# A two-way recurrent scan on TensorE: same-half products in halves of 32 stationary columns, keys and values turned by quadrants

## The chip, the cores and the metric

The kernel runs on one core of a Trainium2 chip. The metric is the device time in microseconds, the median of several runs of the whole program. Inputs and outputs are fp32.

## What is computed

The reference is a chain of four layers on 256 tokens of width 1024: attention and a feed-forward layer, an RWKV-7 time mix and a mixture of experts, latent attention with retention, a gated linear attention, with feed-forward layers between. Only the time mix is touched, and of it the scan: 16 heads of 64 x 64 state, run over 272 tokens forwards and backwards.

```python
def _wkv7_step(S, inp):
    r, w, k, v, kk, a = inp
    sa = jnp.einsum('bhvk,bhk->bhv', S, kk)
    S = S * w[:, :, None, :] - sa[..., None] * (kk * a)[:, :, None, :] + v[..., None] * k[:, :, None, :]
    y = jnp.einsum('bhvk,bhk->bhv', S, r)
    return S, y
...
    _, y_fwd = lax.scan(_wkv7_step, S0, (r_t, tm(decay[0]), tm(kd[0]), v_t, kk_t, tm(a[0])))
    _, y_bwd = lax.scan(_wkv7_step, S0, (r_t, tm(decay[1]), tm(kd[1]), v_t, kk_t, tm(a[1])), reverse=True)
```

## The kernel before

Each engine has a program of its own, written out in full by a Python function (scan_pe, scan_act, scan_dve) with waits on semaphores by hand. The order on an engine is the order in which these functions issue. In the scan, `streams` interleaves three generators on every engine: direction 0, direction 1 and the bonus term, one step of each in turn. The names in the views are tiles: `scan_t` holds the prepared keys and decays and the states, `ring` the work tiles of direction 0, `arena` those of direction 1, `ps` is PSUM, `con` the constants.

The scan is done in chunks of 64 tokens: direction 0 has a first chunk of 16 and four of 64, direction 1 four of 64. Inside a chunk the recurrence is a triangular system. It is solved by doubling: levels 1 to 5 (1 to 3 in the chunk of 16), each with products T (L1454), Y (L1463, not in the last level) and X (L1469). What else TensorE does for a chunk:

- G (L1425): products of keys with keys and queries, in two groups; after the first group Vt (L1434), the values turned from features x tokens to tokens x features by a product with the identity.
- Ut (L1440), then BKt (L1447), the keys of both kinds turned in the same way.
- Z: L1475 within the chunk, and in chunks after the first L1483, which adds the state's part to the same PSUM regions.
- N (L1489), the new values; L1500, the state's part of the output; L1507, the new state; L1515, the output within the chunk.

Sixteen heads are eight tiles i of 128 partitions with two heads p each, head p in partitions 64p to 64p+63. A product of one head uses 64 rows of the array (the half its input is in) and 64 columns (the half its output goes to). `HEADS` is the order i, i+4 with both p; `part(j, i)` sends tiles 4 to 7 to the other half, so that four consecutive products of T, Y, Z's L1475 and N use the four pairs of row half and column half. In X (L1469), L1483 and L1500 input and output are in the same half, so two pairs alternate. Vt and BKt use all 128 rows: one product turns the two heads of a tile, with 64 stationary columns (tokens) and the 128 columns of the identity moving.

`psum.take` deals PSUM banks in turn, aligned to the number asked for. ScalarE copies T, Z, N, Vt and BKt out of PSUM (L1601, L1606, L1612, L1588, L1595), VectorE masks and merges G, Y and X (L1706, L1728, L1732). Every fp32 product is two pairs of a weight load and a matmul record in the trace. The weights of the next stage come through the SP queue, and none of these DMAs stands in the scan.

Of the kernel before, what the change touches and what calls it, by code (L numbers as in the profile page):

```python
# [416 lines left out]
def build(nc, x_d, ws_d, par_d, con_d, dis_d, scn_d, rel_d, ow_d, moe_d, pos_d, out_d):  # L417
# [4 lines left out]
    with ctx:  # L422
# [38 lines left out]
        PS = ps_t[:, :, :]  # L461
# [4 lines left out]
        def con(n):  # L466
            return con_t[:, cc[n][0]:cc[n][0] + cc[n][1]]
# [30 lines left out]
        psum = Banks()  # L498
# [810 lines left out]
        SAME = [(i, p) for i, p in HEADS if i // 4 != p]  # L1309
        OTHER = [(i, p) for i, p in HEADS if i // 4 == p]  # L1310
        TILES = [i + 4 * x for i in range(4) for x in range(2)]

        def own(p, n=64):
            return slice(64 * p, 64 * p + n)

        def part(j, i, n=64):
            return own(j ^ (i // 4), n)
# [7 lines left out]
        def bank(b, i):  # L1325
            return b + i // 4
# [61 lines left out]
        def window(d, j, i, c0):  # L1388
            a = j * AB + i * T0 + c0
            return d.flat[:, a:a + 64]  # L1390

        def scan_pe(w, e):
            w.wait_ge(ac["project"], IN_SCN)

            def steps(n):
                d = dirs[n]
# [15 lines left out]
                for ci, (c0, cn) in enumerate(d.chunks):  # L1412
# [3 lines left out]
                    for q in range(2):  # L1416
# [12 lines left out]
                        if q == 0:  # L1429
                            b, free = psum.take(("Vt", *u))  # L1430
                            w.wait_ge(*free)
                            for i in TILES:
                                x = 128 * (i % 4)
                                last = e.matmul(PS[part(1, i), b, x:x + 128], Vr[:, i, c0:c0 + 64], con("ident"), start=True, stop=True)  # L1434
                            last.then_inc(*pe.on("Vt", *u))
# [8 lines left out]
                    for j in range(2):  # L1444
                        for i in TILES:
                            x = 128 * (i % 4)
                            last = e.matmul(PS[part(j, i), bank(b, i), x:x + 128], window(d, j, i, c0), con("ident"), start=True, stop=True)  # L1447
                    last.then_inc(*pe.on("BKt", *u))
                    yield
                    for lv in range(1, levels(cn)):  # L1450
# [17 lines left out]
                        for i, p in HEADS:  # L1468
                            last = e.matmul(spread(PS[own(p), b:b + 2, :], lv)[:, i], d.T[own(p, cn), i, :], side(d.X[own(p, cn), i, :], lv, d.x_side), start=True, stop=True)  # L1469
# [6 lines left out]
                    if ci:  # L1476
                        last.then_inc(*pe.on())
                        across = pe.now()
                        w.wait_ge(dv["S", n, ci - 1])
                        for i, p in SAME + OTHER:  # L1480
                            if (i, p) == OTHER[0]:
                                w.wait_ge(across)
                            last = e.matmul(PS[own(p, cn), bank(b, i), col(i)], d.AR[own(p), 0, i, cs], d.S[own(p), i, :], start=False, stop=i % 4 == 3)  # L1483
# [14 lines left out]
                    if ci:  # L1498
                        for i, p in STRAIGHT:
                            last = e.matmul(PS[own(p), bank(by, i), col(i, cn)], d.S[own(p), i, :], d.AR[own(p), 1, i, cs], start=i % 4 == 0, stop=False)  # L1500
                        last.then_inc(*pe.on())
                        straight = pe.now()
# [44 lines left out]
        def scan_act(w, e):  # L1547
            w.wait_ge(IN_SCN, IN_PAR)

            def steps(n):  # L1550
# [32 lines left out]
                for ci, (c0, cn) in enumerate(d.chunks):  # L1583
                    u = (n, ci)
                    w.wait_ge(pe["Vt", *u])
                    real = sn("rows")[:, int(cn < C):int(cn < C) + 1]
                    for x in range(2):
                        e.activation(d.NV[own(1 - x), 8 * x:8 * x + 8, :].rearrange("q i t -> q (i t)"), PS[own(1 - x), psum["Vt", *u], :], ACT.Identity, scale=real[own(1 - x)]).then_inc(*ac.on())  # L1588
# [6 lines left out]
                    e.activation(d.BKt.rearrange("q (x i) p t -> q x (i p t)", x=2), PS[:, b:b + 2, :], ACT.Copy).then_inc(*ac.on("BKt", *u))  # L1595
# [2073 lines left out]
```

## Time and profile before

| | us |
|---|---|
| median of 3 runs (lowest, highest) | 2608.56 (2607.54, 2610.41) |
| span of the profiled execution, first to last instruction | 2600.0 |
| TensorE busy, whole span | 2505.0 |
| the scan on TensorE, first product of a chunk to the last | 560 to 795 |
| TensorE, VectorE, ScalarE busy in 616.7 to 782.2 us | 157.95, 85.72, 63.71 |

The profile is of one execution, whose span is 2600.0 us; the runs' times are those of the whole launch and 8.6 us longer in the median. TensorE's busy time is the union of its matmul records, which overlap, so a busy engine may still take short bursts faster or slower. Idle time of an engine is given with what ended it; "issue" means that the profile shows nothing that it waited for. [...]

### The profile page before, as it was taken

The page shows a single profiled execution, that of the slowest core. Times are in us where ns is not written, and L with a number is a line of the kernel's source. Part 1 is how long each engine was busy: PE and PEld are TensorE (multiplying, and loading weights), DVE is VectorE, ACT ScalarE, POOL GpSimd, SP SyncE. Part 2 cuts the span into 40 slices and gives each one's busy share as a digit, 9 for nine tenths or more (in the row PEclk, how much of TensorE's full clock was granted, in tenths as well). Part 3 has the DMA queues.
Part 4 walks back from the last instruction along what each step waited for, and adds up shares of the span by engine and source line. Part 5 has one row for each costly group of instructions (what it writes and reads, how often), then busy time and mean ns, then how long its engine had stood idle before and what let it go on. Part 6 is the DMA issues. An engine that isn't in the chain of part 4 may idle for free.

```text
span 2600.0 us, 54588 instructions
## 1 busy us (share of the span) xinstructions
PE 2505.0 (96%) x23472; PEld 2331.7 (90%) x23472; DVE 1998.4 (77%) x3066; ACT 1537.2 (59%) x2510; POOL 51.9 (2%) x57
## 2 busy tenths in 40 slices
PE   8999999989999999999999999999898899999999
PEld 8779998868887899999999999999897799998999
DVE  5555547775544799999999999999877788675884
ACT  4435434464432677777777777777666566564663
POOL 0001100000000000000000000000003000000000
PEclk9999999978999999999999999999999999998999
DMA  6223452300003599999999999999732255541453
GB/s 246 73 74 122 178 190 100 107 1 4 20 4 115 206 376 337 367 340 368 341 366 335 372 337 370 335 373 345 287 139 105 78 192 191 188 173 50 171 181 128
DMA packets 83257, 538.46 MB, mean 207 GB/s; under 512 B 9488, under 2 KB 9616, under 8 KB 38976
## 3 DMA queue, kind: packets, MB, share of 16 engines
q1 hardware_dynamic: 82368, 530.68, 55.2%
q8 instruction: 186, 3.05, 0.5%
q0 software_dynamic: 640, 4.22, 0.4%
q14 instruction: 63, 0.52, 0.1%
HBM read 533.81 MB, written 1.05 MB: 206 GB/s over the span
## 4 chain that ended last, share of the span: by engine, by line
PE 87%; DVE 7%; ACT 4%; issue 1%; DMA 1%; DVEq 0%; SPq 0%; PEldq 0%; ACTq 0%
PE ps L576 23%; PE ps L577 23%; PE ps L578 23%; PE ps L1469 2%; DVE sl L534 2%; PE ps L591 1%; PE ps L582 1%; PE ps L2000 1%; PE ps L1463 1%; PE ps L1447 1%; PE ps L1454 1%; DMA ring<-ws_d 1%; PE ps L2145 1%; PE ps L1425 1%; PE ps L819 1%
## 5 line engine op out<-in xcount | busy, mean ns | idle before, releaser
L2227 DVE TENSOR_TENSOR sl<-ring,sh 128x1024 fp32r<-128x1024 f32 x613 | 718.1, 1219 | 13.5 <-ACT sh L2185 10.6
L2185 ACT ACTIVATE sh<-ring 128x1024 fp32r<-128x1024 f32 x613 | 609.0, 1061 | 1.3 <-DVE xl L2070 1.3
L576 PE MATMUL ps<-sh,xh 128*128 128x256 f32 (+2 forms) x2012 | 568.0, 282 | 2.1 <-DVE sl L534 1.2
L578 PE MATMUL ps<-sh,xl 128*128 128x256 f32 (+2 forms) x2012 | 567.5, 282 | 0.0
L577 PE MATMUL ps<-sl,xh 128*128 128x256 f32 (+2 forms) x2012 | 567.0, 282 | 0.0
L576 PE MATMUL ps<-xh,sh 128*128 128x256 f32 (+2 forms) x1856 | 538.5, 290 | 22.8 <-DVE sl L534 12.7
L577 PE MATMUL ps<-xl,sh 128*128 128x256 f32 (+2 forms) x1856 | 531.2, 286 | 0.0
L578 PE MATMUL ps<-xh,sl 128*128 128x256 f32 (+2 forms) x1856 | 529.0, 285 | 0.0
L534 DVE TENSOR_TENSOR sl<-ring,sh 128x1024 fp32r<-128x1024 f32 (+1 forms) x341 | 401.0, 1201 | 74.6 <-ACT sh L527 74.3
L527 ACT ACTIVATE sh<-ring 128x1024 fp32r<-128x1024 f32 (+1 forms) x341 | 338.8, 1021 | 111.2 <-PE ps L578 102.8
L576 PEld LDWEIGHTS ps<-sh,xh 128*128 128x128 f32 x2012 | 377.8, 188 | 11.8 <-DVE sl L534 1.6
L577 PEld LDWEIGHTS ps<-sl,xh 128*128 128x128 f32 x2012 | 377.8, 188 | 8.9
L576 PEld LDWEIGHTS ps<-xh,sh 128*128 128x128 f32 (+1 forms) x1856 | 353.3, 190 | 32.6 <-DVE sl L534 12.2
L578 PEld LDWEIGHTS ps<-sh,xl 128*128 128x128 f32 x2012 | 377.8, 188 | 0.3
L578 PEld LDWEIGHTS ps<-xh,sl 128*128 128x128 f32 (+1 forms) x1856 | 354.2, 191 | 0.0
L577 PEld LDWEIGHTS ps<-xl,sh 128*128 128x128 f32 (+1 forms) x1856 | 353.6, 191 | 0.6
L2199 ACT ACTIVATE arena_moe<-ps 128x128 f32<-128x128 f32 x224 | 62.3, 278 | 245.1 <-PE ps L578 244.9
L576 PE MATMUL ps<-sh,moe_h 128*128 128x512 f32 x336 | 145.8, 434 | 1.9 <-DVE kept_l L2232 1.9
L577 PE MATMUL ps<-sl,moe_h 128*128 128x512 f32 x336 | 131.9, 393 | 0.0
L578 PE MATMUL ps<-sh,moe_l 128*128 128x512 f32 x336 | 131.8, 392 | 0.0
L578 PE MATMUL ps<-conv_h,sl 128*128 128x256 f32 x352 | 99.3, 282 | 0.0
L577 PE MATMUL ps<-conv_l,sh 128*128 128x256 f32 x352 | 98.6, 280 | 0.0
(555 smaller groups left out, 3861.1 us busy)
## 6 DMA issues: line engine op xcount, KB each, us to landing
ring<-ws_d SPq DMA_DIRECT2D x229, 1024.0 KB, 7.2
ring<-ws_d SPq DMA_DIRECT2D x80, 1536.0 KB, 6.4
ring<-ws_d SPq DMA_DIRECT2D x225, 512.0 KB, 6.5
ring<-ws_d SPq DMA_DIRECT2D x24, 1408.0 KB, 6.0
ring<-ws_d SPq DMA_DIRECT2D x4, 1256.0 KB, 5.4
ring<-ws_d SPq DMA_DIRECT2D x2, 1088.0 KB, 5.0
scan_t<-scn_d POOLq DMA_DIRECT2D x1, 1844.0 KB, 7.5
ring<-ws_d SPq DMA_DIRECT2D x1, 1248.0 KB, 5.6
```

The source lines that it names most:

```text
L527: e.activation(sh[slot_of[bi]][:, c], ring[:, bi % RING, c], ACT.Copy).then_inc(*ac.on("high", bi, p))
L534: e.tensor_tensor(sl[s][:, c], ring[:, bi % RING, c], f32(sh[s][:, c]), SUB).then_inc(*dv.on("low", bi, p))
L576: e.matmul(out, ah, bh, start=start, stop=False)
L577: e.matmul(out, ah, bl, start=False, stop=False)
L578: return e.matmul(out, al, bh, start=False, stop=stop)
L582: return e.transpose(out, in_, con("ident")[0:k, 0:k])
L591: e.matmul(PS[:, b, 0:256], con("o1024"), con_t[:, WARM:WARM + 256], start=True, stop=True)
L819: e.matmul(PS[:, b, 0:256], v, aT[h % 2][0:kn, kt, :], start=kt == 0, stop=False)
L1469: last = e.matmul(spread(PS[own(p), b:b + 2, :], lv)[:, i], d.T[own(p, cn), i, :], side(d.X[own(p, cn), i, :], lv, d.x_side), start=True, ...
L2185: e.activation(out, raw(u)[:, a:z], ACT.Copy).then_inc(*af.on("high", u, i))
L2199: e.activation(sg_few[u % 2][:, 0, :], PS[:, u % 2, 0:128], ACT.Sigmoid).then_inc(*af.on("sigmoid", u))
L2227: e.tensor_tensor(l, raw(u)[:, a:z], f32(h), SUB).then_inc(s_fd if i < 2 else s_fp, 1)
```

## The change

Vt and BKt no longer use 128 rows: each head is turned alone, by a product on 64 rows with a 64-column identity, in `HEADS` order, and goes to bank b + p, so that Vt takes two banks instead of one. ScalarE's copies of both read two banks with the heads apart. X, L1483 and L1500 cut each product into two with 32 stationary columns each, which write the two quarters of the half. All of L1483 now waits for L1475's last product, where only its second half did. Counts of products: Vt 8 to 16, BKt 16 to 32, X, L1483 and L1500 16 to 32 a burst.

```diff
@@ -1306,12 +1306,12 @@
 
         HEADS = [(i + 4 * x, p) for i in range(4) for x in range(2) for p in range(2)]
         STRAIGHT = [(i, p) for i in range(8) for p in range(2)]
-        SAME = [(i, p) for i, p in HEADS if i // 4 != p]
-        OTHER = [(i, p) for i, p in HEADS if i // 4 == p]
-        TILES = [i + 4 * x for i in range(4) for x in range(2)]
 
         def own(p, n=64):
             return slice(64 * p, 64 * p + n)
+
+        def quarter(p, q):
+            return slice(64 * p + 32 * q, 64 * p + 32 * q + 32)
 
         def part(j, i, n=64):
             return own(j ^ (i // 4), n)
@@ -1427,11 +1427,10 @@
                                         last = e.matmul(out[:, 0, 0:cn], window(d, j, i, c0)[own(p)], d.AR[own(p), 0, i, cs], start=True, stop=True)
                         last.then_inc(*pe.on("G", *u, q))
                         if q == 0:
-                            b, free = psum.take(("Vt", *u))
+                            b, free = psum.take(("Vt", *u), 2)
                             w.wait_ge(*free)
-                            for i in TILES:
-                                x = 128 * (i % 4)
-                                last = e.matmul(PS[part(1, i), b, x:x + 128], Vr[:, i, c0:c0 + 64], con("ident"), start=True, stop=True)
+                            for i, p in HEADS:
+                                last = e.matmul(PS[part(1, i), b + p, col(i)], Vr[own(p), i, c0:c0 + 64], sn("id2")[own(p)], start=True, stop=True)
                             last.then_inc(*pe.on("Vt", *u))
                         yield
                     b, free = psum.take(("Ut", *u), 2)
@@ -1442,9 +1441,8 @@
                     b, free = psum.take(("BKt", *u), 2)
                     w.wait_ge(*free)
                     for j in range(2):
-                        for i in TILES:
-                            x = 128 * (i % 4)
-                            last = e.matmul(PS[part(j, i), bank(b, i), x:x + 128], window(d, j, i, c0), con("ident"), start=True, stop=True)
+                        for i, p in HEADS:
+                            last = e.matmul(PS[part(j, i), b + p, 64 * i:64 * i + 64], window(d, j, i, c0)[own(p)], sn("id2")[own(p)], start=True, stop=True)
                     last.then_inc(*pe.on("BKt", *u))
                     yield
                     for lv in range(1, levels(cn)):
@@ -1466,7 +1464,9 @@
                         b, free = psum.take(("X", *u, lv), 2)
                         w.wait_ge(*free)
                         for i, p in HEADS:
-                            last = e.matmul(spread(PS[own(p), b:b + 2, :], lv)[:, i], d.T[own(p, cn), i, :], side(d.X[own(p, cn), i, :], lv, d.x_side), start=True, stop=True)
+                            for q in range(2):
+                                last = e.matmul(spread(PS[quarter(p, q), b:b + 2, :], lv)[:, i], d.T[own(p, cn), i, 32 * q:32 * q + 32],
+                                                side(d.X[own(p, cn), i, :], lv, d.x_side), start=True, stop=True)
                         last.then_inc(*pe.on("X", *u, lv))
                         yield
                     b, free = psum.take(("Z", *u), 2)
@@ -1477,10 +1477,10 @@
                         last.then_inc(*pe.on())
                         across = pe.now()
                         w.wait_ge(dv["S", n, ci - 1])
-                        for i, p in SAME + OTHER:
-                            if (i, p) == OTHER[0]:
-                                w.wait_ge(across)
-                            last = e.matmul(PS[own(p, cn), bank(b, i), col(i)], d.AR[own(p), 0, i, cs], d.S[own(p), i, :], start=False, stop=i % 4 == 3)
+                        w.wait_ge(across)
+                        for i, p in HEADS:
+                            for q in range(2):
+                                last = e.matmul(PS[quarter(p, q), bank(b, i), col(i)], d.AR[own(p), 0, i, c0 + 32 * q:c0 + 32 * q + 32], d.S[own(p), i, :], start=False, stop=i % 4 == 3)
                     last.then_inc(*pe.on("Z", *u))
                     yield
                     b, free = psum.take(("N", *u), 2)
@@ -1497,7 +1497,8 @@
                         w.wait_ge(*free)
                     if ci:
                         for i, p in STRAIGHT:
-                            last = e.matmul(PS[own(p), bank(by, i), col(i, cn)], d.S[own(p), i, :], d.AR[own(p), 1, i, cs], start=i % 4 == 0, stop=False)
+                            for q in range(2):
+                                last = e.matmul(PS[quarter(p, q), bank(by, i), col(i, cn)], d.S[own(p), i, 32 * q:32 * q + 32], d.AR[own(p), 1, i, cs], start=i % 4 == 0, stop=False)
                         last.then_inc(*pe.on())
                         straight = pe.now()
                     w.wait_ge(ac["N", *u])
@@ -1584,15 +1585,16 @@
                     u = (n, ci)
                     w.wait_ge(pe["Vt", *u])
                     real = sn("rows")[:, int(cn < C):int(cn < C) + 1]
+                    b = psum["Vt", *u]
                     for x in range(2):
-                        e.activation(d.NV[own(1 - x), 8 * x:8 * x + 8, :].rearrange("q i t -> q (i t)"), PS[own(1 - x), psum["Vt", *u], :], ACT.Identity, scale=real[own(1 - x)]).then_inc(*ac.on())
+                        e.activation(d.NV[own(1 - x), 8 * x:8 * x + 8, :].rearrange("q (i p) t -> q p i t", p=2), PS[own(1 - x), b:b + 2, 0:256].rearrange("q p (i t) -> q p i t", i=4), ACT.Identity, scale=real[own(1 - x)]).then_inc(*ac.on())
                     ac.mark("Vt", *u)
                     psum.gone["Vt", *u] = [ac.now()]
                     yield
                     yield
                     w.wait_ge(pe["BKt", *u])
                     b = psum["BKt", *u]
-                    e.activation(d.BKt.rearrange("q (x i) p t -> q x (i p t)", x=2), PS[:, b:b + 2, :], ACT.Copy).then_inc(*ac.on("BKt", *u))
+                    e.activation(d.BKt.rearrange("q i p t -> q p i t"), PS[:, b:b + 2, :].rearrange("q p (i t) -> q p i t", i=8), ACT.Copy).then_inc(*ac.on("BKt", *u))
                     psum.gone["BKt", *u] = [ac.now()]
                     yield
                     for lv in range(1, levels(cn)):
```

TensorE in the middle of the scan, from G of one chunk of direction 0 to the T of the other direction. `ps<-con,arena` are the products with the 128-column identity; a row is of products, not of records. Before:

```order
L1425 MATMUL ps<-scan_t 64x128 x15
L1434 MATMUL ps<-con,arena 64x128 x8
L1463 MATMUL ps<-ring 64x32 [waits s_act_done]
...
L1469 MATMUL ps<-ring 64x32 x16
...
L1440 MATMUL ps<-scan_t 64x64 x16
L1447 MATMUL ps<-con,scan_t 64x128 [waits s_dve_done]
L1447 MATMUL ps<-con,scan_t 64x128 x15
L1469 MATMUL ps<-ring 64x32 [waits s_dve_done,s_act_done]
L1469 MATMUL ps<-ring 64x32 x15
```

The same place after the change:

```order
L1425 MATMUL ps<-scan_t 64x128 x15
L1433 MATMUL ps<-scan_t,arena 64x64 x16
L1461 MATMUL ps<-ring 64x32 [waits s_act_done]
...
L1468 MATMUL ps<-ring 32x32 x32
...
L1439 MATMUL ps<-scan_t 64x64 x16
L1445 MATMUL ps<-scan_t 64x64 [waits s_dve_done]
L1445 MATMUL ps<-scan_t 64x64 x31
L1468 MATMUL ps<-ring 32x32 [waits s_dve_done,s_act_done]
L1468 MATMUL ps<-ring 32x32 x31
```

The order and the waits are the same; the turned values, the turned keys and X have twice the products, of half the size.

TensorE at Z of a later chunk of direction 0, where the state's part is added. Before:

```order
L1475 MATMUL ps<-ring 64x64 x16
L1483 MATMUL ps<-scan_t 64x64 x8
L1483 MATMUL ps<-scan_t 64x64 [waits s_pe_done]
L1483 MATMUL ps<-scan_t 64x64 x7
L1463 MATMUL ps<-arena 64x32 [waits s_dve_done,s_act_done]
```

After:

```order
L1475 MATMUL ps<-ring 64x64 x16
L1483 MATMUL ps<-scan_t 32x64 [waits s_pe_done]
L1483 MATMUL ps<-scan_t 32x64 x31
L1461 MATMUL ps<-arena 64x32 [waits s_dve_done,s_act_done]
```

TensorE's wait for its own products of L1475 has moved ahead of the first eight products of L1483.

## Rows read from the trace of the kernel before

**Rows 1.** The page: busy time of the engines, and the chain that ended last.

```profile
PE 2505.0 (96%) x23472; PEld 2331.7 (90%) x23472; DVE 1998.4 (77%) x3066; ACT 1537.2 (59%) x2510; POOL 51.9 (2%) x57
...
PE 87%; DVE 7%; ACT 4%; issue 1%; DMA 1%; DVEq 0%; SPq 0%; PEldq 0%; ACTq 0%
```

**Rows 2.** Windows of the scan: us, busy us of each engine (records), granted clock.

```profile
586.20:616.70 30.50, 27.65 (x682) 23.68 (x682) 14.25 (x25) 12.23 (x22) 0.00 (x0) 0.72 0.01 3
616.70:782.20 165.50, 157.95 (x5473) 139.99 (x5471) 85.72 (x157) 63.71 (x117) 0.53 (x1) 1.00 0.04 11
782.20:795.40 13.20, 10.56 (x329) 8.57 (x329) 3.73 (x8) 3.52 (x7) 0.00 (x0) 1.00 0.02 4
```

**Rows 3.** TensorE's timeline: start us, us, line, tiles, rows*columns, records, idle before.

```profile
766.02 0.67 PE L1463 MATMUL ps<-ring 64*64 64x32 f32 x32
766.50 1.11 PE L1469 MATMUL ps<-ring 64*64 64x32 f32 x32
767.44 1.11 PE L1469 MATMUL ps<-arena 64*64 64x32 f32 x32
768.48 0.50 PE L1538 MATMUL ps<-arena 128*128 128x272 f32 x1
```

**Rows 4.** TensorE's timeline, stops inside bursts; rows between are left out.

```profile
721.85 0.59 PE L1454 MATMUL ps<-ring 64*64 64x32 f32 x25 [0.75 <-issue]
...
725.43 0.83 PE L1469 MATMUL ps<-ring 64*64 64x32 f32 x23 [0.95 <-issue]
...
729.17 0.97 PE L1507 MATMUL ps<-arena 128*64 128x64 f32 x26 [0.38 <-issue]
```

**Rows 5.** DMA queues in 616.7 to 782.2 us: packets, MB, share.

```profile
q8 instruction: 42, 0.69, 1.8%
```

**Rows 6.** TensorE's timeline around a Vt and a BKt.

```profile
662.68 1.09 PE L1434 MATMUL ps<-con,arena 128*64 128x128 f32 x16
663.70 0.67 PE L1463 MATMUL ps<-arena 64*64 64x32 f32 x32
...
667.86 1.97 PE L1447 MATMUL ps<-con,scan_t 128*64 128x128 f32 x32
669.75 0.67 PE L1463 MATMUL ps<-arena 64*64 64x32 f32 x32
```

**Rows 7.** ScalarE's groups in 616.7 to 782.2 us: busy us, mean ns, idle before.

```profile
L1612 ACT ACTIVATE arena<-ps,scan_t 64x512 f32<-64x512 f32 x8 | 5.5, 683 | 8.2 <-PE ps L1489 8.1
L1588 ACT ACTIVATE ring<-ps,scan_t 64x512 f32<-64x512 f32 x8 | 5.5, 682 | 6.8 <-PE ps L1434 6.7
```

**Rows 8.** TensorE's timeline, bursts of the first chunk with 16 stationary columns.

```profile
568.06 0.41 PE L1440 MATMUL ps<-scan_t 64*16 64x16 f32 x32
...
588.90 0.42 PE L1454 MATMUL ps<-ring 16*16 16x32 f32 x32
```

**Rows 9.** TensorE's groups in 616.7 to 782.2 us.

```profile
L1469 PE MATMUL ps<-arena 64*64 64x32 f32 x576 | 20.5, 219 | 0.1
L1469 PE MATMUL ps<-ring 64*64 64x32 f32 x576 | 20.4, 219 | 0.9 <-issue 0.9
...
L1447 PE MATMUL ps<-con,scan_t 128*64 128x128 f32 x224 | 14.1, 276 | 0.5 <-issue 0.5
...
L1500 PE MATMUL ps<-scan_t 64*64 64x64 f32 x192 | 7.3, 220 | 0.4 <-issue 0.4
L1483 PE MATMUL ps<-scan_t 64*64 64x64 f32 x192 | 6.9, 219 | 0.1
L1434 PE MATMUL ps<-con,arena 128*64 128x128 f32 x98 | 6.8, 279 | 0.0
```

**Rows 10.** Windows of 3.4 us: busy us of each engine, granted clock.

```profile
591.10:594.50 3.40, 2.25 (x98) 2.14 (x100) 1.86 (x4) 1.10 (x3) 0.00 (x0) 1.00 0.02 5
594.50:597.90 3.40, 3.40 (x32) 3.17 (x32) 2.37 (x5) 0.00 (x0) 0.00 (x0) 0.50 0.04 7
...
724.20:727.60 3.40, 2.45 (x116) 2.34 (x114) 0.87 (x2) 0.98 (x2) 0.00 (x0) 1.00 0.02 5
```

## Prediction, made before the changed kernel was run

> **What bounds the kernel now.** I read the page first: TensorE is busy 96% of the span and makes 87% of the chain that ended last [rows 1]. The scan is one stretch of it, so I read the scan by windows. From 616.7 to 782.2 us TensorE is busy 157.95 of 165.5 us at the full clock, while VectorE has 85.72 us and ScalarE 63.71 us of work; before 616.7 us and after 782.2 us there is slack, and half of 586.2 to 616.7 us ran at a reduced clock [rows 2]. A gain or loss of TensorE in the middle stretch is a gain or loss of the kernel.
>
> TensorE has two limits there, and they have to be kept apart. The first is the array. One fp32 product is two LDWEIGHTS and two MATMUL records, so a burst of 16 products is x32. When consecutive products go to four different (row half, column half) tiles, 32 records take 0.48 us (766.02 to 766.50), 15 ns each. The same-half bursts of L1469 touch only two tiles and take 0.94 us (766.50 to 767.44), 29 ns each. When a burst is followed by another shape (768.48) it takes 0.10 us more, 1.04 us [rows 3].
>
> The second limit is the supply of instructions. In the timeline TensorE stops in the middle of bursts, with "issue" as the only releaser. It resumes at 721.85, 725.43 and 729.17 us [rows 4]. Between the first two lie 127 matmul records by the timeline, between the others 128, each with its LDWEIGHTS. The queue named "instruction" of this stretch moved 42 packets and 0.69 MB, 16.4 KB each, while 5473 matmul and 5471 weight records ran [rows 2, 5]; about 260 instructions a packet. So TensorE's program comes in blocks of about 128 matmul records, and where it runs dry one block follows another every 3.58 and 3.74 us, 3.66 us on average, whatever is in it. Five other pairs of neighbouring stops that I measured lie between 3.46 and 3.76 us. At that pace 5473 records, 42.9 blocks, need 157 us; the stretch took 165.5 us. **The middle of the scan already runs within 5% of the rate at which its instructions arrive.**
>
> **The change, part by part.** Everything it touches lies in the scan, and its five edits all double a count of matmul records.
>
> Keys and values by quadrants. BKt (L1447) took 1.89 us for 32 records (667.86 to 669.75), with a change of shape ahead of it (0.10 us). It becomes 64 records over four tiles in the shape of its neighbours: 64 x 15 ns = 0.96 us. That is 1.03 us less of array time, nine times: 9.3 us. Vt (L1434) took 1.02 us (662.68 to 663.70) and 0.10 us of change; it becomes 32 records, 0.48 us: 0.64 us less, nine times, 5.8 us [rows 6]. ScalarE reads Vt from two banks instead of one; its copies of N already have that form and take 683 ns, against 682 ns for Vt now [rows 7], so nothing is added. BKt's copy moves the same 1024 columns and is off the path. Vt takes two banks instead of one, but the next product asked for an even bank anyway.
>
> Halves of 32 columns. L1469 is issued 43 times, L1483 and L1500 seven times each: 57 bursts, each from 32 to 64 records. No row has exactly this shape. The nearest are two bursts of the first chunk on tiles of 16 columns, L1440 with 64 rows and L1454 with 16 rows and the same 32 moving columns: 32 records in 0.41 and 0.42 us, of which the last record alone is 0.19 us, so that starts are about 7 ns apart [rows 8]. By that 64 take 0.47 us, with a change of shape ahead and one behind some 0.70 us, against about 0.95 us now: 0.25 us less, 14.3 us over 57. The other end is that a record gets no cheaper than the 15 ns of a four-tile burst: 0.96 us and two changes, 1.16 us, 12 us more in all. I take the first, because these rows too are bursts of small tiles. The wait on "across" now stands ahead of all of L1483, so TensorE waits for its own last L1475 product, at most one record's 220 ns, 1.5 us over seven; behind it stand L1483 and then ScalarE's Z copy.
>
> Array time alone would thus fall by 9.3 + 5.8 + 14.3 - 1.5 = **28 us**, or by 1.6 us at the other end.
>
> Instructions. In 616.7 to 782.2 us the doubled groups are L1469 (two groups of 576), L1483 and L1500 (192 each), L1434 (98) and L1447 (224): 1858 records more [rows 9]. 5473 + 1858 = 7331 records are 57.5 blocks of 127.5, and at 3.66 us a block they need **210.4 us where 165.5 us stand now: 44.9 us more**. Would they be hidden behind work? The array time of the stretch is 165.5 less 7.5 us that it stood idle less 23 us of savings (7 BKt, 6 Vt, 48 of the 57 bursts), 135 us, 2.35 us a block. That is under 3.66 us, so the blocks set the time and the 28 us vanish in longer stops. With the cycle at 3.46 or 3.76 us the term is 33.4 or 50.7 us.
>
> Outside that stretch the supply hardly binds. 586.2 to 616.7 us holds 682 records and would hold 874, 6.9 blocks, 25.1 us, in 30.5 us; 782.2 to 795.4 us holds 329 and would hold 457, 3.6 blocks, 13.1 us, in 13.2 us [rows 2]. The shorter BKt and Vt of the first chunks save something there and denser stops cost something: I take 0, with -4 and +3 us as ends.
>
> **Sum.** 2600.0 + 44.9 = 2644.9 us of span. The runs' median is 8.6 us above the profiled span, which lies outside the program's instructions: **2653 us**. With the ends of the two terms the forecast's own range is 2638 to 2663 us. About 0.2% (5 us) is what a measurement of this kernel can tell from no change.
>
> [...]
>
> [...]
>
> **Rivals.**
> *The supply doesn't bind (faster).* If blocks could be fetched further ahead once many short ones follow each other, the array's 28 us would count: 2581 us, up to 2607 us with dear quarter records. It decides as soon as the cycle falls under 2.9 us (165.5 / 57.5). For it: most blocks now take longer than the cycle, so the steady starved state is seen only in short runs. Against it: in the longest run, four stops from 718.09 (inside a burst) to 729.17 us, the cycle doesn't shrink.
> *The supply binds in part.* A cycle of about 3.2 us gives 184 us, +19: 2628 us.
> *The clock falls too (slower still).* With 2.35 us of work in 3.66 us, TensorE is busy about two thirds. [...] At half clock a block needs 4.7 us instead of 3.66; if half the blocks fall there, 29 x 1.04 = 30 us come on top: 2683 us.
>
> **How the numbers follow.** Forecast 0.62; clock 0.17; supply in part 0.08; supply not binding 0.13, of which 0.10 is faster and 0.03 within 5 us. One case in a hundred of the partial supply lands within 5 us too. So faster 0.10, same 0.04, slower 0.86. The range 2628 to 2690 us holds the forecast, the partial supply and the clock case to its middle, and leaves out the 0.13 and the upper part of the clock case.
>
> **What would show it.** Right: stops with "issue" as releaser in nearly every block of the scan, their resumes 3.5 to 3.8 us apart; 57 or 58 instruction packets between the same places of the program in about 210 us; BKt's 64 records (L1445) in 1 us and the halves' 64 of L1468 in 0.6 to 0.7 us where no stop falls in them; TensorE's busy time in the scan lower while the stretch is longer. Wrong: resumes under 3 us apart, or a scan that ends before 790 us. L1468 bursts of 1.1 us or more would mean dear quarter records; a clock of 0.50 after 620 us is the third rival.

## The result, and the profile after

| | before | after |
|---|---|---|
| median (lowest, highest), us | 2608.05 (2602.03, 2610.41) | 2653.41 (2650.07, 2661.58) |
| ratio of the runs' times, with its 95% interval | | 1.0183 (1.0162 to 1.0203) |
| span of the profiled execution, us | 2600.0 | 2648.2 |
| the scan from 586.2 / 585.7 us to its end, us | 209.2 | 262.3 |
| matmul records in it | 6480 | 8657 |
| its instruction packets | 50 | 68 |
| mean granted clock of TensorE, whole span | 0.979 | 0.969 |

The changed kernel is slower by 1.8%. The page of the changed kernel answers [rows 1]: engines with busy us and instruction counts, the granted clock (PEclk, in tenths of the full one) in 40 slices, the instruction queue (packets, MB), the chain.

```profile
PE 2506.0 (95%) x25728; PEld 2325.4 (88%) x25728; DVE 1998.3 (75%) x3066; ACT 1536.6 (58%) x2510; POOL 51.8 (2%) x57
...
PEclk9989999987989999999999999999999999999999
...
q8 instruction: 204, 3.34, 0.5%
...
PE 86%; DVE 7%; ACT 4%; issue 3%; DMA 1%; DVEq 0%; SPq 0%; PEldq 0%; ACTq 0%
```

TensorE's busy time is 2506.0 us, 1 us more than before, while the span is 48.2 us longer and the share of "issue" in the chain grew from 1 to 3%. The added time is idle time for which the profile shows no releaser. The kernel fetched 18 instruction packets more than before (186 there), for 2256 records more.

Windows of the scan of the changed kernel, between the same places of the program as [rows 2] (us; busy us and records of PE, PEld, DVE, ACT, POOL; granted clock; DMA share; GB/s):

```profile
585.70:613.00 27.30, 25.00 (x875) 21.61 (x879) 13.69 (x25) 12.27 (x22) 0.00 (x0) 0.62 0.02 5
613.00:833.70 220.70, 166.28 (x7338) 141.79 (x7330) 85.33 (x157) 63.82 (x117) 0.53 (x1) 0.89 0.03 9
833.70:848.00 14.30, 11.00 (x468) 8.34 (x457) 3.74 (x8) 3.52 (x7) 0.03 (x1) 0.99 0.02 5
```

The middle stretch grew from 165.5 to 220.7 us, with the same 85 and 64 us on VectorE and ScalarE. TensorE is busy in 166.3 of it, and the granted clock is 0.89, where it was 1.00. The instruction queue of that stretch answers [rows 5]:

```profile
q8 instruction: 57, 0.93, 1.8%
```

7338 records in 57 packets are 129 a packet. TensorE's timeline of the changed kernel, stops as in [rows 4] (start us, us, line, tiles, records, idle before):

```profile
718.26 0.28 PE L1439 MATMUL ps<-scan_t 64*64 64x64 f32 x4 [1.61 <-issue]
...
722.16 0.26 PE L1468 MATMUL ps<-ring 64*32 64x32 f32 x7 [2.01 <-issue]
...
725.91 0.31 PE L1483 MATMUL ps<-scan_t 64*32 64x64 f32 x7 [1.27 <-issue]
...
729.75 0.29 PE L1489 MATMUL ps<-ring 64*64 64x64 f32 x5 [1.73 <-issue]
...
733.49 0.45 PE L1508 MATMUL ps<-ring 128*64 128x64 f32 x8 [0.98 <-issue]
...
736.96 0.45 PE L1516 MATMUL ps<-ring 128*64 128x64 f32 x8 [0.89 <-issue]
```

The stops come at whatever line is next, 3.90, 3.75, 3.84, 3.74 and 3.47 us apart, and 0.9 to 2.0 us long where those of [rows 4] were 0.4 to 1.0 us.

The trace also has the packets of the instruction queue one by one, and they show what ends the stops. Packets of this queue landed at 716.78, 720.64, 724.54, 728.33, 732.25 and 735.69 us, and the six resumes above follow 1.2 to 1.6 us behind. In the whole middle stretch there are 41 stops of 0.3 us or more for which the profile has no releaser; they hold 51.4 of the 54.4 us in which TensorE stood idle, and every one of them ends 1.2 to 1.6 us after such a packet landed. In the kernel before all 8 such stops of the middle stretch (5.0 us) do the same. No two packets of the queue overlap there. Twenty-six pairs of neighbouring stops lie one block apart at the full clock, and their cycle has three parts: the next packet starts 1.27 us after the resume in the mean, takes 1.14 us, and TensorE resumes 1.38 us after it has landed, 3.80 us in all (3.36 to 4.04).

The new bursts where no stop falls into them, in three pieces of the same timeline:

```profile
649.77 1.15 PE L1445 MATMUL ps<-scan_t 64*64 64x64 f32 x62
650.85 0.37 PE L1468 MATMUL ps<-ring 64*32 64x32 f32 x19
...
692.04 0.68 PE L1475 MATMUL ps<-arena 64*64 64x64 f32 x29
692.81 1.10 PE L1483 MATMUL ps<-scan_t 64*32 64x64 f32 x64
693.84 0.55 PE L1461 MATMUL ps<-ring 64*64 64x32 f32 x24
...
734.47 0.75 PE L1468 MATMUL ps<-arena 64*32 64x32 f32 x64
735.16 0.45 PE L1516 MATMUL ps<-ring 128*64 128x64 f32 x8
```

A BKt takes 1.1 us (649.72 for its first two records to 650.85) where [rows 6] have 1.89. An X takes 0.69 us where [rows 3] have 0.94 to 1.04. L1483 takes 1.03 us, 0.88 us from its first to its last start; the whole products took 0.90 us from first to last start, so it gains nothing.

### The profile page after: what moved, and what is told of

Read it like the earlier page. It is cut to its first block, busy times and chain, and to the rows that moved or that the text cites. A ratio compares the mean times of both kernels' runs of the same rounds, so it can differ in the third digit from the quotient of the medians.

```text
span 2648.2 us, 59102 instructions
## 1 busy us (share of the span) xinstructions
PE 2506.0 (95%) x25728; PEld 2325.4 (88%) x25728; DVE 1998.3 (75%) x3066; ACT 1536.6 (58%) x2510; POOL 51.8 (2%) x57
## 4 chain that ended last, share of the span: by engine, by line
PE 86%; DVE 7%; ACT 4%; issue 3%; DMA 1%; DVEq 0%; SPq 0%; PEldq 0%; ACTq 0%
PE ps L576 23%; PE ps L577 23%; PE ps L578 23%; DVE sl L534 2%; PE ps L1468 1%; PE ps L582 1%; PE ps L591 1%; PE ps L2002 1%; PE ps L1452 1%; PE ps L1461 1%; PE ps L1425 1%; PE ps L819 1%; PE ps L2147 1%; DMA ring<-ws_d 1%; PE ps L1403 0%
## 5 line engine op out<-in xcount | busy, mean ns | idle before, releaser
L2229 DVE TENSOR_TENSOR sl<-ring,sh 128x1024 fp32r<-128x1024 f32 x613 | 718.3, 1220 | 13.2 <-ACT sh L2187 10.3
```

The costliest lines, as they stand in the source:

```text
L2229: e.tensor_tensor(l, raw(u)[:, a:z], f32(h), SUB).then_inc(s_fd if i < 2 else s_fp, 1)
```

## Experiments

Each kernel was timed in alternation with the kernel before on the same chip: the first four kernels on one chip, the short G, the wide X and the first chunks on a second, the other three on a third. Kernels of different chips are compared by their ratios to the kernel before (median 2606.9, 2607.1 and 2606.1 us). The ratios are those of the alternated runs and not the quotients of the medians; the two differ by up to 0.2%. Intervals are 95%. The supply theory is the forecast's: where TensorE starves, time is blocks of some 128 records times their cycle. The array theory is its first rival. The third is the granted clock.

**One half of the change each.** The turns alone (Vt and BKt by quadrants, the rest as before; of the edit, Vt is shown):

```diff
-                            for i in TILES:
-                                x = 128 * (i % 4)
-                                last = e.matmul(PS[part(1, i), b, x:x + 128], Vr[:, i, c0:c0 + 64], con("ident"), start=True, stop=True)
+                            for i, p in HEADS:
+                                last = e.matmul(PS[part(1, i), b + p, col(i)], Vr[own(p), i, c0:c0 + 64], sn("id2")[own(p)], start=True, stop=True)
```

> The changed kernel with L1468 (X), L1483 and L1501 as before (64 stationary columns): only keys and values are turned by quadrants. Supply of instructions sets the time: the middle of the scan has 322 matmul records more than before, 5795, 45.5 blocks, 166 to 174 us for 165.5 us, and the first chunks save about 3 us: 2606 to 2614 us against 2608 us for the kernel before. Rival, the array's time sets it and the quarter products are what costs: the turns save their 15 us of array time, 2593 us.

Measured: 2626.2 us (2616.08 to 2631.66), ratio 1.0061 (1.0040 to 1.0082). Both theories missed; it is slower than either allowed. The halves alone (X, L1483 and L1500 as in the changed kernel, turns as before; X is shown):

```diff
-                            last = e.matmul(spread(PS[own(p), b:b + 2, :], lv)[:, i], d.T[own(p, cn), i, :], side(d.X[own(p, cn), i, :], lv, d.x_side), start=True, stop=True)
+                            for q in range(2):
+                                last = e.matmul(spread(PS[quarter(p, q), b:b + 2, :], lv)[:, i], d.T[own(p, cn), i, 32 * q:32 * q + 32],
+                                                side(d.X[own(p, cn), i, :], lv, d.x_side), start=True, stop=True)
```

> The kernel before with only X, L1483 and L1500 cut in halves of 32 stationary columns. Supply: 7009 records in the middle, 55.0 blocks, 201 to 211 us, so +36 to +46 us: 2643 to 2653 us, that is not slower than the full change, although the turns' 15 us of array time are spent again. Rival, array time: the full change plus 15 us, 2668 us.

Measured: 2645.52 us (2637.26 to 2648.69), ratio 1.0153 (1.0136 to 1.0171), as the supply theory has it and 22 us under the array theory. Its scan took 244.9 us with 64 packets.

**More records, and fewer.** The changed kernel with a third, repeated product in each pair of X:

```diff
-                            for q in range(2):
+                            for q in (0, 1, 0):
                                 last = e.matmul(spread(PS[quarter(p, q), b:b + 2, :], lv)[:, i], d.T[own(p, cn), i, 32 * q:32 * q + 32],
```

> The changed kernel with the first quarter product of every pair in X issued a second time (96 records a burst instead of 64, same values written again; no part of the computation is left out). 1376 records more, at 9 ns each 12 us of array time. Supply: 10.8 blocks x 3.7 us = +40 us, 2693 us. Rival, array time: +12 us, 2665 us.

Measured: 2695.59 us (2691.82 to 2697.56), ratio 1.0341 (1.0321 to 1.0360). Against the changed kernel's 1.0183 that is 41 us for 1376 records or 10.8 blocks more, 3.8 us each; the supply theory had 2693, the array theory 2665. The changed kernel with L1483 and L1501 whole again (L1501 is shown):

```diff
-                            for q in range(2):
-                                last = e.matmul(PS[quarter(p, q), bank(by, i), col(i, cn)], d.S[own(p), i, 32 * q:32 * q + 32], d.AR[own(p), 1, i, cs], start=i % 4 == 0, stop=False)
+                            last = e.matmul(PS[own(p), bank(by, i), col(i, cn)], d.S[own(p), i, :], d.AR[own(p), 1, i, cs], start=i % 4 == 0, stop=False)
```

> The changed kernel with L1483 and L1501 whole again (64 stationary columns), X still in halves. The array takes the same time for both forms (0.88 us from first to last start in the changed kernel and 0.90 us before). Supply: 448 records fewer, 3.5 blocks, -13 us: 2640 us. Rival, array time: within 3 us of 2653 us.

Measured: 2642.0 us (2635.76 to 2651.02), ratio 1.0147 (1.0122 to 1.0172). 448 records fewer, 3.5 blocks, give 9 us by the ratios; 13 us were expected.

**The same records, other array work.** If the records set the time, work can be taken out or put in under them. One kernel cuts G's moving columns from 128 to 64, which leaves the query half of G out of the computation; the other doubles X's from 32 to 64 (`whole` gives slots of 64 columns, of which VectorE takes the half it needs):

```diff
-                                        last = e.matmul(out, window(d, j, i, c0)[own(p)], d.AR[own(p), :, i, cs], start=True, stop=True)
+                                        last = e.matmul(out[:, 0, 0:cn], window(d, j, i, c0)[own(p)], d.AR[own(p), 0, i, cs], start=True, stop=True)
```

> The kernel after, with one change: every product of G moves 64 columns instead of 128, so the query half of G is left out of the computation. The number of records, their order and all waits stay; only the array's work falls, by my estimate from the bursts of G by about 7 us over the whole scan. Supply: the time of the scan is the number of blocks times their cycle, so the 7 us vanish in longer stops: 2653 us, at most 4 us off it either way, with bursts of G that end sooner and resumes 3.7 to 3.9 us apart as before; if the idler array also spends more time at half clock, 2 to 8 us slower. Array theory (the quarter shape and the work of the array set the time): 7 us faster, 2646 us.

```diff
-                                last = e.matmul(spread(PS[quarter(p, q), b:b + 2, :], lv)[:, i], d.T[own(p, cn), i, 32 * q:32 * q + 32],
-                                                side(d.X[own(p, cn), i, :], lv, d.x_side), start=True, stop=True)
+                                last = e.matmul(whole(PS[quarter(p, q), b:b + 2, :])[:, i], d.T[own(p, cn), i, 32 * q:32 * q + 32],
+                                                d.X[own(p, cn), i, :], start=True, stop=True)
```

> The kernel after, with one change: the quarter products of X (L1471) move all 64 columns of X instead of the 32 that are needed. The number of records stays; each of the 43 bursts should go from about 0.56 us to 0.90 us (64 records at 14 ns instead of 8.9), 14 us more array work in all. Supply: the 14 us fit into the stops, 2653 us within 6 us, and if the busier array keeps its full clock for longer, up to 10 us faster than that. Array theory: 14 us slower, 2667 us. If the clock and not the number of records made the kernel slower than before, this kernel should win back most of it and come out near 2630 us or below.

Measured: 2653.45 us with the short G (ratio 1.0188, 1.0169 to 1.0207) and 2652.43 us with the wide X (1.0189, 1.0168 to 1.0210). The changed kernel has 1.0183. The scan of the short-G kernel, then of the wide-X kernel, by windows:

```profile
584.50:847.20 262.70, 206.98 (x8656) 174.84 (x8657) 103.34 (x189) 79.58 (x146) 0.53 (x1) 0.81 0.03 8
```

```profile
585.60:842.10 256.50, 205.52 (x8658) 175.09 (x8657) 103.15 (x189) 78.92 (x146) 0.56 (x2) 0.93 0.03 9
```

TensorE's groups in the scan of the changed kernel (records, busy us, mean ns, idle before):

```profile
L1425 PE MATMUL ps<-scan_t 64*64 64x128 f32 x512 | 20.1, 289 | 4.7 <-issue 2.7 <-DVE scan_t L1700 1.5 <-DVE arena L1759 0.4
L1468 PE MATMUL ps<-arena 64*32 64x32 f32 x1280 | 18.8, 207 | 10.6 <-issue 10.5
L1468 PE MATMUL ps<-ring 64*32 64x32 f32 x1280 | 18.2, 206 | 8.0 <-issue 7.5 <-ACT ring L1603 0.5
```

The group of G in the short-G kernel, and those of X in the wide-X kernel:

```profile
L1425 PE MATMUL ps<-scan_t 64*64 64x64 f32 x512 | 13.1, 238 | 4.0 <-issue 3.0 <-DVE scan_t L1700 0.5 <-DVE arena L1759 0.4
```

```profile
L1471 PE MATMUL ps<-ring 64*32 64x64 f32 x1280 | 27.2, 237 | 4.5 <-issue 3.9 <-ACT ring L1606 0.5
L1471 PE MATMUL ps<-arena 64*32 64x64 f32 x1280 | 26.8, 230 | 9.7 <-issue 9.6
```

G fell from 20.1 to 13.1 us, the 7 us that were meant, and the time did not move. X grew from 37.0 to 54.0 us and the time did not move either. 24 us of array work lie between these two kernels and 1 us of time; the one with more work has the shorter scan in its profile. With the chips' own ratios the three kernels agree within 0.1%: the number of records sets the time. In the profiles the granted clock follows the array's work: 0.81 in the scan with the short G, 0.87 in the changed kernel, 0.93 with the wide X. Over the whole span their runs have 0.960 to 0.964, 0.964 to 0.969 and 0.970 to 0.976. With the same records, the more columns the products move, the higher the clock.

**Why the turns alone lose: the clock.** In the profile of the turns alone the scan took 230.9 us with 54 packets and a granted clock of 0.86, against 209.2 us, 50 packets and 0.96 before. TensorE's timeline there, and windows around the place:

```profile
775.39 0.46 PE L1464 MATMUL ps<-arena 64*64 64x32 f32 x16
777.64 0.37 PE L1464 MATMUL ps<-arena 64*64 64x32 f32 x11 [1.80 <-issue]
```

```profile
774.30:777.70 3.40, 1.60 (x109) 1.49 (x100) 2.37 (x5) 1.31 (x2) 0.00 (x0) 1.00 0.02 5
777.90:781.30 3.40, 3.40 (x46) 2.63 (x40) 0.87 (x2) 0.00 (x0) 0.00 (x0) 0.50 0.02 5
...
784.70:798.40 13.70, 13.70 (x203) 10.20 (x202) 2.79 (x5) 1.77 (x4) 0.00 (x0) 0.50 0.01 1
```

BKt is done early, the block runs out, 128 records after the last resume at 773.73, TensorE stops for 1.80 us, and it comes back to a granted clock of 0.50 for 20.5 us (777.9 to 798.4) in which it has work all the time.

How much that costs can be read from the two scans. With the turns alone 64.9 us of the scan were at half clock, and 1344 records ran in them; at the pace of the rest of that scan (166.0 us for 5520 records) these would have taken 40.4 us, so the low clock accounts for 24 us. In the kernel before the same account gives 7 us (17.1 us with 316 records, the rest 192.1 us for 6161). So 17 of the 21.7 us between the two scans stand at half clock.

Three kernels tested the clock as the cause: two here, and the last kernel of the next part. First the turns alone, with X's products moving all 64 columns (X as one product per head; the same records as the turns alone):

```diff
-                            last = e.matmul(spread(PS[own(p), b:b + 2, :], lv)[:, i], d.T[own(p, cn), i, :], side(d.X[own(p, cn), i, :], lv, d.x_side), start=True, stop=True)
+                            last = e.matmul(whole(PS[own(p), b:b + 2, :])[:, i], d.T[own(p, cn), i, :], d.X[own(p, cn), i, :], start=True, stop=True)
```

> The kernel of e1 (keys and values turned by quadrants, X whole), with X's products moving all 64 columns instead of 32. The counts of records are those of e1, and a burst of X costs the same 29 ns a record or more, so neither supply nor array time gives a gain; both expect what e1 gave, 2626 us, or 1 to 10 us more if the wider products are slower. The clock's theory says that e1 was slow because its array had less to do and its granted clock fell (0.969 in the mean of its runs, 0.977 in those of before, and within the runs of before 0.001 of mean clock goes with 2.4 us): with more work per record the clock should come back to 0.973 or above and the time to 2606 to 2616 us.

Measured: 2612.26 us (2606.15 to 2627.38), inside what the clock's theory had, ratio 1.0030 (1.0011 to 1.0049), where the turns alone had 1.0061: twice the moving columns in X, and by the ratios 8 us less time (14 us by the medians). The intervals just overlap, so that anything came back is likely and not certain, and half of the loss is the best reading of how much. The mean clock of its ten runs is 0.975, against 0.969. The last stage of the scan, from the last Ut on, by windows: before, the turns alone, the turns with wide X.

```profile
758.20:795.40 37.20, 34.41 (x1010) 27.41 (x1003) 14.20 (x28) 10.83 (x22) 0.00 (x0) 1.00 0.01 4
```

```profile
773.90:821.20 47.30, 42.70 (x1039) 33.30 (x1034) 13.41 (x28) 10.82 (x22) 0.06 (x1) 0.78 0.01 3
```

```profile
766.70:804.90 38.20, 33.64 (x1038) 26.67 (x1037) 13.18 (x28) 10.83 (x22) 0.00 (x0) 1.00 0.02 4
```

With the same 1038 records, the stage takes 38.2 us at 1.00 and 47.3 us at 0.78. Second, BKt alone by quadrants (Vt as before):

```diff
-                        for i in TILES:
-                            x = 128 * (i % 4)
-                            last = e.matmul(PS[part(j, i), bank(b, i), x:x + 128], window(d, j, i, c0), con("ident"), start=True, stop=True)
+                        for i, p in HEADS:
+                            last = e.matmul(PS[part(j, i), b + p, 64 * i:64 * i + 64], window(d, j, i, c0)[own(p)], sn("id2")[own(p)], start=True, stop=True)
```

> The kernel before with BKt alone turned by quadrants: 256 records and 2 blocks more in the scan, 9.3 us less array time. Array theory: 2598 us. Supply without the clock: between 2598 and 2606 us, as the middle chunks already take what the supply gives. The clock's theory: its mean falls below 0.974 in most runs and the time is 2610 to 2622 us, less than e1's loss of 18 us because the array loses less work.

Measured: 2627.39 us (2607.16 to 2642.26), ratio 1.0063 (1.0033 to 1.0093); all three theories missed the time, though in six of seven runs the mean clock fell below 0.974 as the clock's theory had it. That is as much as both turns, not less: the size of the loss is not proportional to records or work. But its seven runs follow their clock: 2607 us at 0.976, 2615 at 0.972, 2624 to 2639 at 0.967 to 0.969, 2642 at 0.961.

**Where the forms do pay.** The kernel before, with the changed forms of Vt, BKt and X only where `u[1] == 0`, the first chunk of each direction (X is shown):

```diff
+                        if early(u):
+                            for i, p in HEADS:
+                                for q in range(2):
+                                    last = e.matmul(spread(PS[quarter(p, q), b:b + 2, :], lv)[:, i], d.T[own(p, cn), i, 32 * q:32 * q + 32],
+                                                    side(d.X[own(p, cn), i, :], lv, d.x_side), start=True, stop=True)
+                        else:
```

> The kernel before, with the changed forms of Vt, BKt and X in the first chunk of each direction only (stages in which TensorE waits for other engines or has spare supply). About 300 records more, in a stretch that in the changed kernel took 3 to 4 us less than before. Supply: no stop is added there, 3 us faster, 2604 us; but if every 127 records cost 3.7 us even there, 2 blocks more, 5 to 8 us slower. Array theory (savings of about 1 us for BKt, 0.6 us for Vt and 0.25 us for each X burst, two chunks): 4 to 5 us faster, 2602 us. The clock's theory: a change of a few us either way with the half-clock time of the scan, which the trace will show.

Measured: 2602.23 us over 12 runs, ratio 0.9982 (0.9969 to 0.9994). It is 5 us faster than the kernel before, just clear of noise. Supply had 2604 us and array time 2602 us, too close to be told apart. The windows of these chunks, from the first Ut to the third, before and in this kernel:

```profile
568.10:621.00 52.90, 45.59 (x997) 38.77 (x996) 30.44 (x47) 24.18 (x39) 0.00 (x0) 0.72 0.01 3
```

```profile
573.30:621.30 48.00, 39.09 (x1269) 32.62 (x1268) 30.43 (x47) 24.11 (x39) 0.00 (x0) 0.71 0.01 4
```

4.9 us less at nearly the same clock, with 272 records more: 1269 records are 10 blocks, 37 us at the starved pace, and the stretch is longer than that because TensorE waits for ScalarE and VectorE in it, 8.5 us in all. The last kernel is this one with X's products 64 columns wide in every chunk.

> The kernel of e6 (changed forms in the first chunks only), with all of X's products moving 64 columns instead of 32, in every chunk. Records as in e6. Supply and array time expect e6's 2602 us again, or up to 10 us more where the wider products are slower. The clock's theory: the half-clock stretch around 591 to 621 us shrinks, the mean clock rises from 0.976 towards 0.980, and the time falls to 2592 to 2600 us.

Measured: 2602.28 us, ratio 0.9987 (0.9974 to 1.0000). The mean clock was higher, 0.978 against 0.976, but the time did not fall to the 2592 to 2600 us of the clock's theory, which missed here. Wide X is no gain where the clock is up anyway. The ratio is again on the side of a gain over the kernel before, for the same forms in the first chunks.

**All scans side by side**, each from the profile of its kernel:

| kernel | records | packets | scan, us | us a packet | clock |
|---|---|---|---|---|---|
| before | 6480 | 50 | 209.2 | 4.18 | 0.96 |
| first chunks | 6753 | 53 | 207.4 | 3.91 | 0.97 |
| first chunks, wide X | 6752 | 53 | 211.5 | 3.99 | 0.95 |
| BKt alone | 6736 | 53 | 235.7 | 4.45 | 0.87 |
| turns, wide X | 6864 | 54 | 218.8 | 4.05 | 0.95 |
| turns | 6865 | 54 | 230.9 | 4.28 | 0.86 |
| halves | 8273 | 64 | 244.9 | 3.83 | 0.94 |
| X halves, turns | 8209 | 64 | 245.7 | 3.84 | 0.89 |
| wide X | 8658 | 68 | 256.5 | 3.77 | 0.93 |
| after | 8657 | 68 | 262.3 | 3.86 | 0.87 |
| short G | 8656 | 68 | 262.7 | 3.86 | 0.81 |
| third product | 10000 | 78 | 295.6 | 3.79 | 0.87 |

From 64 packets on the time follows the packets, at 3.8 us each, and the clock moves it by some 6 us. Under that the packets no longer tell the time: with 53 or 54 of them the scan takes from 207.4 to 235.7 us, short where the clock is 0.95 or more and long where it is 0.86 or 0.87. The turns with the wide X take 12 us less than the turns with less work.

## Why the prediction was right

**The sum.** 2653 us were forecast and 2653.41 measured, but some of that is luck, because terms that were off cancel. Of the span, 2644.9 us were forecast and 2648.2 measured: the middle stretch was 10.3 us longer than forecast, the head 3.2 us shorter, the tail 1.1 us longer and the rest of the program 4.9 us shorter. The runs' median then lies 5.2 us above the profiled span and not 8.6 us.

**The supply term** carried the result. The count was right: 7331 records and 57.5 blocks forecast, 7338 records and 57 packets found. The stretch took 220.7 us instead of 210.4. Of it 172.9 us were at the full clock, with 5967 records, 3.71 us for every 128; the forecast had 3.66 for its block. The other 47.8 us, in six pieces, were at half clock, with 1358 records, 4.50 us for every 128. So the pace at full clock was right within 0.1 us, which makes 2 to 3 us over the stretch, and about 8 of the missing 10 us are the clock's. Right behind a stop the cycle is longer than that mean, 3.80 us over the 26 pairs of stops.

**The array term** of -28 us was to vanish in the stops, and it did: the short G and the wide X show it, the change alone would not have. Its parts were sized unequally. Turns: 1.1 us for BKt where 0.96 was forecast; the change of shape, which the prediction left out, is still there. X: 0.69 us, forecast 0.70, right. L1483 and L1501: mis-sized. I took the price of X for them, but they move 64 columns: 1.03 us instead of 0.70, no better than the whole products, some 5 us of array time over 14 bursts, which the stops hid. The row that I had for it moved 32 or 16 columns. The step on "across" is right in kind: from 692.04 the last product of L1475 is waited for, and L1483 starts about 0.3 us after it started; 7 times that is 2 us, forecast 1.5.

**Head, tail, rest.** Head 27.3 us where 30.5 stood: -3.2, near the lower end of the forecast's -4 to +3, and the first-chunks kernel shows it as a gain of its own. Tail +1.1 us, within the same bounds. The other 4.9 us are 0.5 us ahead of the scan's first G and 4.4 us behind the scan, in code that was not touched (1804.6 and 1800.2 us, clock 0.99 in both); where these come from was not looked into. The 8.6 us "outside the program's instructions" was wrong as a step. All runs of the kernel before lie only 1.8 us above their own span; the rest was a profiled execution some 6 us faster than the median. Adding the difference was right, for the median against one execution, but not for the reason given.

**The rivals.** Supply not binding, 2581 us: refuted, no two neighbouring stops of the changed kernel lie less than 3.36 us apart, and their mean is 3.80. Supply in part, with a cycle of 3.2 us: refuted by the same. The clock falls too: this happened, but in another size than forecast. I had half the blocks at half clock and 30 us; it was 47.8 us of the stretch with 10.6 blocks, and 8 us. Its price per block, 4.7 us, measured 4.50. It should have been a term of the sum and not only a rival. [rows 10] spoke for this rival: TensorE was busy 66% of the 3.4 us ahead of a clock of 0.50 and 72% around 724 us, where the clock stayed at 1.00, and the new load, 2.35 of 3.66 us or 64%, is below both.

The clock deserved more for another reason. 51 runs of the kernel before, on three chips, have mean clocks from 0.974 to 0.980, and their times go from 2613 to 2599 us, 2.0 us for each 0.001. The turns alone have 0.9688 where before has 0.9773: 17 us by that slope, and they are 19 us slower in the mean. So without the clock the turns alone would cost about nothing, and the account of the two scans comes near that: 4 of the 21.7 us are left. The turns with wide X, at 0.975, are 7 us slower in the mean, of which their clock makes 4. In neither do the 15 us of array work appear as a gain, as the supply theory has it. That slope is a relation between runs, not an intervention; the wide X, which puts work in and changes no record, is the intervention, and it gave about half of the loss back.

What stays open: why BKt alone loses as much as both turns. Its clock accounts for the time of each run, but why it fell as often as theirs was not shown. And no run changed the supply itself: that it is blocks to be fetched, and not a pace of single records, rests on the times of the queue's packets and stops.

## What to carry to other kernels

Count records before nanoseconds: where TensorE has short instructions, divide its matmul records by the instruction packets of the same stretch, look for stops with "issue" at unrelated lines in equal steps (3.36 to 4.04 us in the changed kernel), and where there are many of them treat packets times that step as a floor: here, from 64 packets on, at 3.8 us each, a difference of 24 us in array work moved the time by 1 us. Splitting an instruction paid here only where the engine waits for others anyway, in the first chunks. And a saving that turns into stops can cost more than nothing: with the turns alone the scan had 64.9 us at half clock, against 17.1 us before, and took 21.7 us more.

## What the runs showed of the hardware

- A block of about 128 matmul records with their weight loads takes TensorE some 3.7 to 3.8 us to get when it starves, in kernels whose instructions do different amounts of work. At the full clock neighbouring stops lie 3.80 us apart in the changed kernel (mean of 26), 3.68 with the third product (30), 3.72 with the short G (12) and 3.73 with the wide X (23). One packet of the instruction queue lies between any two of them, and the next one starts only 1.0 to 1.8 us after TensorE has resumed.
- Every fp32 product of the scan leaves two weight loads and two matmul records: X (L1469) has 43 bursts of 16 products in the kernel before, and the trace has 1376 LDWEIGHTS and 1376 MATMUL. Where the program's order goes through four pairs of row half and column half, 32 records without a stop at the full clock start 14.5 ns apart (T and Y, 36 bursts); where it alternates between two pairs, 28.9 ns apart (X, 13 bursts). Rows, columns and moving columns are the same in both, 64*64 and 32. On 16 stationary columns the last record of a burst takes 0.18 to 0.19 us (L1440 and L1454 of [rows 8]).
- Products of quarters (32 stationary columns): 64 records with 32 moving columns start 8.9 ns apart at full clock (X in the changed kernel, 18 bursts without a stop), with 64 moving columns 14.0 ns (wide X, 20 bursts). From its last start to the next burst it is 0.13 us more (0.69 less 0.56), with 64 moving columns 0.15 us.
- The granted clock went with the array's work, not only with the presence of instructions: with equal records 0.9625, 0.9662 and 0.9737 over the whole span in the means of the runs (short G, changed kernel, wide X). At half clock a burst of X in the turns-only kernel takes 1.71 us (787.28 to 788.99) instead of 1.06:

```profile
766.12 1.13 PE L1470 MATMUL ps<-arena 64*64 64x32 f32 x32
767.18 1.15 PE L1516 MATMUL ps<-ring 128*64 128x64 f32 x32
...
787.28 1.91 PE L1470 MATMUL ps<-ring 64*64 64x32 f32 x32
788.99 1.91 PE L1470 MATMUL ps<-arena 64*64 64x32 f32 x32
```
